# The emission order of a whole decoder-layer kernel: program order replaced by a list scheduler

## The reference

```python
a = rmsnorm(h, in_norm_g)
proj = a @ w_in                       # pooling channels u, queries q, three pairs of keys/values, gates
y_pool = pool_mixer(u, pool_w, pool_scale)     # trailing means over 2/4/8/16 tokens, minus the token
kcmp, vcmp = compress_blocks(kc, ...), compress_blocks(vc, ...)
o_cmp = softmax(q kcmp) @ vcmp                 # compressed branch; its weights pick 16 blocks of 64 keys
o_sel = softmax over the picked blocks of (ks, vs)
o_win = softmax over the last 512 keys of (kw, vw)
o = g0 * o_cmp + g1 * o_sel + g2 * o_win
h = h + concat(y_pool, o) @ w_out
h = h + (silu(rmsnorm(h) @ w_gate) * (rmsnorm(h) @ w_up)) @ w_down
h = h + (p @ w_ple_proj) * sigmoid(rmsnorm(h) @ w_ple_gate)
out = rmsnorm(h, final_norm_g)
```

## Time and profile before

| | us |
|---|---|
| median of six runs | 1875.0 |
| undisturbed runs, lowest to highest | 1872.95 to 1875.78 |
| the profiled execution, its own time | 1874.59 |
| its span, slowest core (core 4) | 1873.0 |

### The profile page before, as it was taken

How to read it: one execution, slowest core, us unless ns; L and a number is a source line. 1 busy time by engine, 2 the same in 40 slices (tenths; PEclk the granted TensorE clock), 3 DMA queues, 4 the chain that set the end, 5 groups by cost and what they waited for, 6 DMA issues and landing times.

```text
span 1873.0 us, 23525 instructions; the slowest of 8 cores (1861.6 to 1873.0 us)
## 1 busy us (share of the span) xinstructions
PE 1676.4 (90%) x8496; PEld 796.6 (43%) x8496; DVE 714.5 (38%) x1426; ACT 397.3 (21%) x695; POOL 65.0 (3%) x133
## 2 busy tenths in 40 slices
PE   0898899777777899899999999999999999986995
PEld 0355454334444454344444444444444444432442
DVE  2766523866665543611122111121111221056665
ACT  2333211244454551200000000000000000022332
POOL 1000000000000000000000000000000001000000
PEclk9998888989999999999999999999999999988997
DMA  9632333311152209238441284430663404934022
GB/s 195 158 98 74 61 59 59 62 24 24 32 128 46 46 12 212 47 65 138 90 79 34 46 135 76 83 68 15 113 120 69 89 1 79 170 56 90 0 91 90
DMA packets 22114, 146.65 MB, mean 78 GB/s; under 512 B 3376, under 2 KB 3760, under 8 KB 7152
## 3 DMA queue, kind: packets, MB, share of 16 engines
q0 software_dynamic: 15120, 110.14, 33.8%
q1 hardware_dynamic: 6880, 35.01, 5.8%
HBM read 246.88 MB, written 8.39 MB: 136 GB/s over the span
## 4 chain that ended last, share of the span: by engine, by line
PE 81%; DVE 9%; issue 4%; DMA 3%; ACT 2%; DVEq 0%; SPq 0%; ACTq 0%
PE ps L260 70%; PE ps L573 5%; DMA arena<-x 3%; PE ps L707 2%; PE ps L717 2%; DVE arena L688 1%; PE ps L710 1%; DVE arena L599 1%; DVE arena L356 1%; DVE arena L657 1%; DVE arena L346 1%; ACT arena L345 1%; PE ps L351 1%; DVE arena L398 0%; DVE arena L399 0%
## 5 line engine op out<-in xcount | busy, mean ns | idle before, releaser
L260 PE MATMUL ps<-arena 128*128 128x512 bf16 (+3 forms) x6464 | 1369.4, 375 | 5.6 <-DVE arena L356 2.6
L260 PEld LDWEIGHTS ps<-arena 128*128 128x128 bf16 x6464 | 634.4, 99 | 746.9 <-issue 66.7
L918 DVE TENSOR_TENSOR arena<-ps,arena 128x512 bf16<-128x512 f32 x88 | 60.8, 692 | 533.9 <-PE ps L260 533.9
L917 ACT ACTIVATE arena<-ps 128x512 f32<-128x512 f32 x88 | 52.6, 598 | 796.1 <-PE ps L260 796.1
L573 PE MATMUL ps<-arena 128*128 128x512 bf16 (+1 forms) x672 | 201.6, 374 | 21.7 <-DVE arena L770 6.5
L657 DVE TENSOR_TENSOR arena<-ps,arena 128x512 f32<-128x512 f32 x160 | 110.3, 689 | 212.2 <-PE ps L260 199.3
L711 ACT ACTIVATE arena<-ps 128x512 bf16<-128x512 f32 x216 | 127.2, 595 | 131.4 <-PE ps L707 54.3
L346 DVE TENSOR_TENSOR arena<-arena 128x512 f32<-128x512 f32 x150 | 103.6, 691 | 122.3 <-ACT arena L345 117.5
L345 ACT ACTIVATE arena<-arena 128x512 f32<-128x512 f32 x150 | 92.7, 628 | 223.5 <-DVE arena L657 112.1
L356 DVE SCALAR_TENSOR_TENSOR arena<-arena 128x512 bf16<-128x512 f32 (+1 forms) x160 | 106.9, 746 | 38.0 <-ACT arena L353 38.0
L351 PE MATMUL ps<-arena 128*128 128x512 f32 x20 | 17.8, 988 | 95.6 <-DVE arena L346 95.6
(11 more groups left out here) (99 smaller groups left out, 507.6 us busy)
## 6 DMA issues: line engine op xcount, KB each, us to landing
arena<-x SPq DMA_DIRECT2D x24, 1024.0 KB, 13.4
arena<-wgate POOLq DMA_DIRECT2D x22, 1024.0 KB, 10.1
arena<-wup POOLq DMA_DIRECT2D x22, 1024.0 KB, 12.3
arena<-wdown POOLq DMA_DIRECT2D x12, 1536.0 KB, 17.4
arena<-wout POOLq DMA_DIRECT2D x12, 1024.0 KB, 9.5
arena<-wpg POOLq DMA_DIRECT2D x4, 2048.0 KB, 14.9
out<-arena SPq DMA_DIRECT2D x16, 512.0 KB, 3.0
arena<-wkv POOLq DMA_DIRECT2D x5, 1024.0 KB, 35.0
```

The costliest lines, as they stand in the source:

```text
L260: PE(lambda e, i=i, lhsT=lhsT, rhs=rhs: e.matmul(out, lhsT=lhsT, rhs=rhs, start=(i == 0), stop=(i == n - 1)), reads(i), [PB[pb]])
L918: DVE(lambda e, pu=pu, sg=sg, ci=ci, h=h: e.tensor_tensor(out=hf[ci][:, h * 512:(h + 1) * 512], in0=ps[pu][:], in1=sg, op=ALU.mult), [PB[p ...
```

## The change

`Sched` keeps one list of all instructions instead of five, and `emit` first calls a new function, `order`. It plays the program through on a clock of its own. `cost` gives each instruction a duration by engine, size and type; loads go one after the other at 330 bytes per nanosecond with 2 us of latency. The engine that is free first takes, of its instructions whose inputs are done on that clock, the one with the smallest `key`, which is the place in the program text; if none is ready, it takes the one that becomes ready first. The five lists that come out are emitted as before. The dependences are those of the program text, so buffers and banks change hands in the same sequence; `_add` now also notes those between two PE instructions. `bias` is 0 throughout.

Apart from that, the two places that took the filler's other bank for a transpose (in `c1_stages`, the selection mask; in `combine`, the output) take the next bank of `srot`.

```diff
@@ class Sched, _add
-        op.idx = len(self.ops[eng])
+        op.key = len(self.ops) + self.bias
...
-        self.ops[eng].append(op)
+        self.ops.append(op)
@@ new functions
+    def cost(o):
+        p = _Probe()
+        o.fn(p)
+        aps = [x for x in list(p.a) + list(p.k.values()) if hasattr(x, "shape")]
+        n = max([_free(x) for x in aps] + [1])
+        out = p.k.get("out", p.a[0] if p.a else None)
+        o.nbytes = 0
+        o.lat = 0.0
+        if o.dma_key is not None:
+            o.nbytes = 4 * n * out.shape[0]
+            o.busy = 0.6 if o.eng == "pool" else 0.1
+        elif o.eng == "pe":
+            n = _free(out) if p.name == "matmul" else 128
+            fp32 = p.name == "matmul" and p.k["rhs"].dtype == F32
+            o.busy = max(0.03, n / 2400.0 * (4 if fp32 else 1))
+            o.lat = 0.17
+        elif o.eng == "act":
+            o.busy = 0.17 + n / 1250.0
+            o.lat = 0.06
+        elif o.eng == "dve":
+            if any(x.tensor.name.startswith("ps") for x in aps):
+                o.busy = 0.15 + n / 960.0
+            elif all(x.dtype == BF16 for x in aps):
+                o.busy = 0.1 + n / 1920.0
+            else:
+                o.busy = 0.09 + n / 960.0 * (8 if p.name == "reciprocal" else 1)
+        elif p.name == "nop":
+            o.busy = 0.05
+        else:
+            o.busy = 0.3 + n / 480.0
+
+    def order(self):
+        for i, o in enumerate(self.ops):
+            self.cost(o)
+            o.succ = []
+            o.left = len(o.deps)
+            o.ready = 0.0
+        for o in self.ops:
+            for d in o.deps:
+                d.succ.append(o)
+        free = {e: 0.0 for e in ENGS}
+        soon = {e: [] for e in ENGS}
+        avail = {e: [] for e in ENGS}
+        out = {e: [] for e in ENGS}
+        dma_free = 0.0
+        for i, o in enumerate(self.ops):
+            o.idx = i
+            if o.left == 0:
+                heapq.heappush(soon[o.eng], (0.0, o.key, i))
+        left = len(self.ops)
+        while left:
+            best, eng = None, None
+            for e in ENGS:
+                t = free[e]
+                if not avail[e]:
+                    if not soon[e]:
+                        continue
+                    t = max(t, soon[e][0][0])
+                if best is None or t < best:
+                    best, eng = t, e
+            while soon[eng] and soon[eng][0][0] <= best:
+                _, k, i = heapq.heappop(soon[eng])
+                heapq.heappush(avail[eng], (k, i))
+            o = self.ops[heapq.heappop(avail[eng])[1]]
+            o.start = best
+            free[eng] = best + o.busy
+            o.done = free[eng] + o.lat
+            if o.dma_key is not None:
+                dma_free = max(dma_free, free[eng] + 1.5) + o.nbytes / 330e3
+                o.done = dma_free + 0.5
+            out[eng].append(o)
+            left -= 1
+            for n in o.succ:
+                n.ready = max(n.ready, o.done + (0.0 if n.eng == "pe" and eng == "pe" and o.dma_key is None else self.SEM))
+                if n.eng == "pe" and eng == "pe":
+                    n.ready = max(n.ready, free[eng])
+                n.left -= 1
+                if n.left == 0:
+                    heapq.heappush(soon[n.eng], (n.ready, n.key, n.idx))
+        return out
@@ emit
+        ops = self.order()
...
-            for o in self.ops[e]:
+            for o in ops[e]:
+                o.deps = [d for d in o.deps if not (d.eng == "pe" and o.eng == "pe" and d.dma_key is None)]
...
@@ c1_stages, s3
-            tb = other_bank()
+            tb = srot()
             PE(lambda e: e.transpose(out=psb[tb][0:32, 0:128], in_=sel, identity=ident), [Bsel, B_tri], [PB[tb]])
```

More of the change, by code:

```diff
@@ L1 @@
+import heapq
 import numpy as np
@@ L31, with __getattr__, call, _free @@
 class Op:
-    __slots__ = ("eng", "fn", "deps", "signal", "sigval", "dma_key", "dma_val", "idx")
+    __slots__ = ("eng", "fn", "deps", "signal", "sigval", "dma_key", "dma_val", "idx", "key", "busy", "lat", "nbytes", "done", "succ", "left", "ready", "start")
+class _Probe:
+    def __getattr__(self, name):
+        def call(*a, **k):
+            self.name, self.a, self.k = name, a, k
+        return call
+def _free(ap):
+    return int(np.prod(ap.shape[1:])) if hasattr(ap, "shape") else 0
 class Sched:
+    SEM = 0.1
     def __init__(self):
-        self.ops = {e: [] for e in ENGS}
-        self.dma_cnt = {}
+        self.ops = []
         self.placed = []
+        self.bias = 0
     def buf(self, name, off=None, nbytes=0):
@@ L75, in _add @@
             if b.excl:
-                deps.extend(t for t in b.readers if t[1] != eng)
+                deps.extend(t for t in b.readers if t.eng != eng)
         for b in writes:
@@ L81, in _add @@
             deps.extend(b.readers)
[L82 to L89, removed]
+        op.deps = set(deps)
         for b in reads:
-            b.readers.append(tok)
+            b.readers.append(op)
         for b in writes:
-            b.last_w = tok
+            b.last_w = op
             b.readers = []
-        self.ops[eng].append(op)
+        self.ops.append(op)
         return op
@@ L102, in dma @@
         return self._add(eng, fn, list(reads), list(writes), dma_key=key)
+    @staticmethod
+    def cost(o):
[28 more added lines that the diff above has]
+            o.busy = 0.3 + n / 480.0
@@ L104, in emit @@
     def emit(self, nc, stack):
+        ops = self.order()
+        cnt = {}
         for e in ENGS:
-            for o in self.ops[e]:
+            for o in ops[e]:
+                o.deps = [d for d in o.deps if not (d.eng == "pe" and o.eng == "pe" and d.dma_key is None)]
                 for d in o.deps:
-                    if d[0] == "eng":
-                        self.ops[d[1]][d[2]].signal = True
+                    if d.dma_key is None:
+                        d.signal = True
+                if o.dma_key is not None:
+                    cnt[o.dma_key] = cnt.get(o.dma_key, 0) + 16
+                    o.dma_val = cnt[o.dma_key]
@@ L118, in emit @@
                 esem[e] = stack.enter_context(nc.semaphore(f"s_{e}"))
-        dsem = {k: stack.enter_context(nc.semaphore(f"d_{k}")) for k in self.dma_cnt}
+        dsem = {k: stack.enter_context(nc.semaphore(f"d_{k}")) for k in cnt}
         block = stack.enter_context(nc.Block())
-        ops = self.ops
         def run(e, engobj):
@@ L127, in run @@
                 for d in o.deps:
[L128 to L131, removed]
-                    else:
-                        sem = dsem[d[1]]
-                        val = d[2]
-                        key = ("d", d[1])
+                    if d.dma_key is None:
+                        sem, val, key = esem[d.eng], d.sigval, ("e", d.eng)
+                    else:
+                        sem, val, key = dsem[d.dma_key], d.dma_val, ("d", d.dma_key)
                     if need.get(key, (None, -1))[1] < val:
```

## The result

The changed kernel takes 1731.21 us (median of 8 executions, 1730.55 to 1732.32) against 1875.26: a ratio of 0.9235 [0.9226, 0.9244]. That is 144 us less where the sum forecast 92, and 4 us under the low end of the range. It is where the rival "everything goes" stood, which had 0.07.

What follows compares the result with a forecast made beforehand. PE, busy 90%, was held by its place in the program, with DVE setting attention's first part. Terms 22 + 8 + 28 + 10 + 4 + 20 = 92 us off 1874.6 gave 1783 us; range 1735 to 1855.

Steps and rivals of the forecast that it cites:

- everything goes: Rival: attention's two parts overlap, PE stays dense, clock at 1.00; 120 to 143 us less, around 1745; chance 0.07.
- The norm stalls: First projection blocks: PE no longer held at the norm's ones-matmul L351; 22 us gained, bounds 8 to 31.
- the late load at the start: Start: fifth load of x lands at 62.3 us, ACT and DVE stand at its squares; costed 0, bound 15 us.
- The small load: Before attention: DVE runs rope evacuations instead of standing at the vcmp copy behind c_overlap's load; 8 us, 0 to 12.56.
- Attention, first part: 350 to 535 us: DVE sets the length, at best 147 us; 28 us gained, bounds 6 and 38.
- Attention, second part: 535 to 705 us: PE sets the end, about 140 us at full clock; 10 us gained, bounds 0 and 30.
- The turns: To the FFN: 4 us gained (0 to 8); to the last stage: 20 us (8 to 24).
- SwiGLU, gated input, tail: SwiGLU: PE dense, nothing won, changed load order costed at 0; tail: a chain of true dependences that stays.
- ACT's tables: ACT's order ignores the loaded function table; two more loads per norm would be 26 us of ACT, adding nothing.
- DVE keeps what it has: Rival: the order's DVE times too short, attention gives 0 to 10 us; about 35 us less, 1840; chance 0.20.
- Slower: Rival: 24 transposes in score banks delay scores; loses from 3.8 us each, 1908 at full price; chance 0.09.

Runs made afterwards that it cites:

- start_landed: Changed kernel, but the first five loads of x land on the invented clock at their traced times; 1714.73 us, ratio 0.9160.
- no_mix: Changed kernel, but on the invented clock a sum's next matmul may follow at once, without the 0.17 us latency; 1714.71 us, ratio 0.9159.
- the old banks: Changed kernel, but the two transposes take the filler's other bank again, the scheduler alone; 1725.39 us, ratio 0.9215.
- the raised prices: Changed kernel, but DVE's prices on the invented clock raised to the trace's durations and the gap behind each; 1728.83 us, ratio 0.9232.
- mix_in_text: Kernel before, in program order, but the compressions' strided matmuls written alternately with those of the query pieces behind them; 1876.4 us, ratio 1.0016.

## Why the prediction was wrong, step by step

**The norm stalls: right by two errors.** From the first to the fourth norm it took 158.2 us before (42.33 to 200.57) and takes 136.5 after: 21.7 gained, 22 forecast. But start_landed has 122.2 (41.92 to 164.14), so the stalls themselves were worth 36, above the bound of 31, and the late load at the start took 14.3 back: the first block even grew, from 50.4 to 55.9. The prediction saw this hazard and bounded it at 15; it costed it at 0 because "PE has seven banks of 3.4 us in hand". PE did go on, but DVE, which the paragraph on the stalls has late "with hardly any reserve", hadn't caught up by the second norm, where PE stood 5.59 us for it.

**The small load: the size right, the place not.** From the fourth norm to the first score 151.0 became 144.3: 6.7, forecast 8. But PE hardly stood there before. These are the windows of before and after, and PE's two waits in before for the rope evacuations (L399) that had piled up on DVE:

```profile
200.57:351.60 151.03, 148.83 (x758) 73.09 (x758) 66.59 (x108) 22.98 (x50) 8.34 (x19) 0.89 0.41 66
...
178.73:323.00 144.27, 143.62 (x765) 72.26 (x776) 75.12 (x120) 23.40 (x53) 7.25 (x17) 1.00 0.40 63
...
351.63 0.38 PE L732 MATMUL ps<-arena 128*128 128x512 bf16 x1 [2.23 <-DVE arena L399]
...
357.52 3.28 PE L573 MATMUL ps<-arena 128*128 128x512 bf16 x8 [4.60 <-DVE arena L399]
```

At most the 2.23 us belong to the hazard; the rest of the 6.7 is PE's busy time at a clock of 1.00 and not 0.89, which the sum didn't price. The other 4.60 us lie inside attention, and their gain is counted there.

**Attention, first part: the step that failed.** I took DVE's floor as 147, its busy time and 25 us of gaps "which no order removes", and three quarters of the way to it for wrong prices. The stage took 138.1. Of the 44.9 us, 18.9 are DVE's waits (38.2 to 19.3, where I had said under 15), 11.0 its busy time, and 15.0 the gaps, which are 24.2 before and 9.2 after: 0.07 and 0.026 us for each instruction. The busy time isn't less work: the durations of DVE's instructions in this stage add up to 126.7 before and 126.1 after, but an independent one starts up to 0.08 us before the one ahead ends, and 16.6 us overlap after where 6.1 did before. So 25 of the 44.9 us are spacing that I held fixed. Before, a chain of small dependent instructions stood together on DVE, each 0.1 us after the end of the one before:

```profile
432.87 0.18 DVE L679 RECIPROCAL arena<-arena 128x4 f32<-128x4 f32 x1
433.15 0.17 DVE L682 TENSOR_TENSOR arena<-arena 128x4 f32<-128x4 f32 x1
433.42 1.26 DVE L688 SCALAR_TENSOR_TENSOR arena<-ps,arena 128x128 f32<-128x128 f32 x3
```

After, the order puts independent work between them, and the gaps close:

```profile
386.89 0.75 DVE L690 TENSOR_TENSOR arena<-arena 128x572 f32<-128x572 f32 x1
387.57 0.17 DVE L770 RECIPROCAL arena<-arena 128x4 f32<-128x4 f32 x1
387.75 0.75 DVE L690 TENSOR_TENSOR arena<-arena 128x564 f32<-128x564 f32 x1
388.42 0.16 DVE L773 TENSOR_TENSOR arena<-arena 128x4 f32<-128x4 f32 x1
388.61 0.69 DVE L696 SCALAR_TENSOR_TENSOR arena<-arena 128x512 bf16<-128x512 f32 x1
```

So most of the gaps were a property of the order and not of the instructions. The discount was wrong too: I had compared the prices with durations, not with DVE's pace on independent work, and higher prices gained about 2 us in all. Nor was 147 the bound: PE's length, which I had as "about 120 at the full clock" and set aside, is nearer to what the stage can reach (124.4 in no_mix).

**Attention, second part: the other half of the failure.** I saw that PE sets the end and that its dense length was about 140, and then took a third of the way because the filler might be used up early. It wasn't: in after, each 15 us of this part hold 23 to 27 filler matmuls until the end at 604. PE came to 141.51 busy of 143.00.

**Why single waits misled me.** PE and DVE wait for each other in attention. With DVE in text order PE's freedom is worth 10 us, 39 with ACT's; with PE in text order that of all the others is worth 28; with PE and DVE free it is 78. The forecast priced each stage at what one engine's waits would give and then took a discount for the other; "near full at once" was my argument against "everything goes", and it is what happened.

**The turns.** 3.1 and 24.5, forecast 4 and 20; the second by the mechanism described (no wait at L442, outputs evacuated in alternation).

**SwiGLU, gated input, tail: right at 0.** The loads' new order cost nothing (841.4).

**ACT's tables.** Thirteen loads of 1283 ns where there were nine, 5 us more of ACT, and the gated input, where three of them lie, stays at 120.0. The Trainium skill (ScalarE: Activation LUTs, "Table sets: the hidden batching unit") has about 2.7 us for a load. The trace of after doesn't agree, and it decides here: with its input there, a load starts 0.02 us behind the instruction ahead, and the next one 0.01 us behind the load.

```profile
1586.94 0.60 ACT L1071 ACTIVATE arena<-ps 128x512 f32<-128x512 f32 x1
1587.56 1.28 ACT L443 ACT_TABLE_LOAD   x1
1588.85 0.69 ACT L443 ACTIVATE arena<-ps,arena 128x512 f32<-128x512 f32 x1
```

**The rivals.** "DVE keeps what it has" did not come from short prices: with DVE's halved, attention still gives 43 us, and the 1804.18 lie under the rival's 1815; attention gives nothing only where all prices are alike. "Slower" had its sign right and its size wrong: 0.5 us a transpose, and not the 3.8 from which it decides.

**What stays open**: why the old banks, the raised prices and the landings don't add, though each alone is no loss; with every edit the list scheduler draws a new order, and attention moves by up to 11 us with it. And whether it is the late ends of alternated sums that cost the 13.7 us of no_mix.

## What to carry to other kernels

When two engines wait for each other in turn, price the reordering at the larger of their dense times (here PE's 140 us in the second part and its 120 in the first, where no_mix reached 124), not at a share of one engine's waits, and test it with each engine free alone and both free. Gaps between dependent instructions on one engine count as removable if independent work can stand between them, and part of its busy time too, since the durations of independent instructions overlap. A low granted clock costs what the matmuls at it lose by their starts; here the strided ones lost next to nothing. An order made on an invented clock is only as good as its few far-off prices: DVE prices 10 to 20% under the durations cost 2 us at most and a further fifth 22, and one load taken as 3 us that took 55 cost 16.

## What the runs showed of the hardware

- DVE starts an independent instruction about when the one before ends, or up to 0.08 us ahead of that (387.57 behind one that lasts from 386.89 to 387.64; 1568.78 behind 1568.18 to 1568.87), and a dependent small one 0.10 us after it (433.15 behind 432.87 to 433.05).
- In the compression the mean granted clock was 0.69, a mix of 2.4 and 1.2 GHz, with the strided matmuls in a row (no_mix, 236 to 285 us), and 1.00 with matmuls of the queries between them (after); PE counts as busy for all of the 49 us in the one and for 48.72 in the other. The strided matmuls kept nearly the same pace at either clock: 0.46 us each in a row in no_mix, 0.43 alternated at 1.00 in mix_in_text.
- A 1 MB load of x that was issued at 7.2 us, among the first loads of weights, took 55.1 us.
- A load of an ACT function table took 1.28 us, with no more than 0.02 us before it and 0.01 behind it where ACT had its input (after, 1586.94 to 1588.85).
